# One-core inference step with expert retrieval: the lead-in before the first gather is rebuilt

## The chip, the cores and the metric

The kernel runs on one core of one Trainium2 chip. The metric is the time of one execution in device microseconds (us). Three executions of the kernel before took 3244.26, 3246.60 and 3248.41 us; their median, 3246.6 us, is the time before. One more execution was recorded by the profiler.

Names used for the engines: PE is TensorE (PEld its weight loads), DVE is VectorE, ACT is ScalarE, POOL is GpSimd, SP is SyncE, which only issues DMAs here.

## The reference, cut to what matters

1024 prompt tokens and 64 sample tokens, each 1024 wide, go through one layer, all in float32:

```
x <- LN1(alpha*x + Mixer(x))
x <- LN2(alpha*x + PEER(x))
Mixer: one projection (1024 -> 2048: lru_x 512, lru_gate 512, sc_B, sc_C, sc_x, mem_q 256 each)
  A (512): conv of width 4 -> gated linear recurrence over time -> * gelu(gate)
  B (256): y = B * conv3(C * x_sc)
  C (256, 4 heads): softmax attention into 256 memory tokens (k, v = mem @ w_mem_kv)
  RMSNorm of each group, concatenation, one output projection (1024 -> 1024)
PEER: 8 heads; scores against 2 x 128 keys, top 16 of each half, top 16 of the 256 sums;
  every token gathers 16 experts per head: rows u and v of 1024 floats out of 16384
  out = sum over experts of softmax(score) * gelu(x . u) * v
```

Outputs are x of all tokens, the keys and values of the prompt's memory, and the last states of convolutions and recurrence.

## The kernel before

Tokens are cut into tiles of 128 (8 of the prompt, one half-filled of the sample). **The main loop** runs over 1088 slots. A slot is one gather: POOL issues an indirect DMA (L698) that brings u and v rows for 128 pairs of token and expert, 1 MB, into one of 8 ring buffers of `arena` (`RING`). DVE takes the dot product with the token's x (L1567), ACT makes gelu and weight (L1166 to L1175), and PE adds the weighted v rows into the tile's sum (`combine`, L972, two matmuls). Gather n waits for `used`, the end of `combine(n - 8)`. `replicate` (L956, copied by ACT at L1144) spreads x for the dots, once for 2 slots in the first groups. The indices of a gather come from `keyscores` (L921), `route` on DVE (top 16s, L1449 to L1507), `select` on PE (L941) and `copy_idx` (L1514), for a unit of two heads at a time.

**The mixer** is computed in three blocks of three tiles. Blocks 1 and 2 are mixed into the slots of the main loop. Block 0 (tiles 0 to 2, 384 tokens) has to come first, since no gather can start without x after LN1: its work is the lead-in. It is cut into named stages: `half` and `lx`, `lg`, `qp`, `sx`, `sb`, `sC` (the two halves of a projection of 128 columns, L725), `kv`, `kt`, `kk`, `kc` (memory keys and values), `cv` (convolution), `gr`, `gi`, `sr`, `si`, `ta`, `ra`, `rc`, `sd`, `re` (gates and recurrence), `as`, `mx`, `ex`, `nz`, `at`, `tc`, `av`, `ty` (attention, six rounds r: tile r // 2, half of the heads), `sh` (group B), `sq`, `nm`, `rm`, `no` (RMSNorm of one group: squares, sum by a matmul with ones, root, scaling), `oa`, `ob`, `op` (output projection of one tile and half of the columns; `oa` and `ob` are its parts for tile 0, L849), `z` (residual sum, L1419), `l1`, `dv`, `l2` (layer norm, L1425 to L1437), `xt`, `xe` (transposes, L880), `w0`, `wa`, `wq` (query projections, one side of 16 each, L891: `w0` for tile 0 alone, `wa` and `wq` for more tiles), and `K0`, `T0`, `E0`, `S0`, `I0`, `G0`, `R0`, `C0` (key scores, routing, selection and replication of the first unit).

**The order** is written by hand: `put(engine, step, block, name, arg)` adds a stage to an engine's list, and each list is sorted by step. Steps below 0 (from `LEAD`, -200) are the lead-in, run one stage after another; steps from 0 are slots, and there `PE_PACE` and `DVE_PACE` say how many slots pass between two pieces of a stage. A stage waits by semaphore for the stages that it reads. SP's list holds the loads: weights of a stage go through three buffers `win`, so the load of one waits for the stage three before it (`weight`). ACT issues the first three weights and memT, wkv before its own work.

```
put("pe", v(38), "op", (1, 0))
for side in range(8):
    put("pe", v(40 if side < 4 else 49), "w0", side)
put("pe", v(42), "K0")
for n, (ti, half) in enumerate(((1, 1), (2, 0), (2, 1))):
    put("pe", v(43 + n // 2), "op", (ti, half))
put("pe", v(46), "S0")
```

So all six output projections and both halves of tile 0's stand ahead of `S0` on PE. `w_out` (4 MB) lies in ring buffers 4 to 7, and gather 4 waits for the last `op`.

## Time and profile before

| | |
|---|---|
| median of three executions | 3246.6 us (3244.26 to 3248.41) |
| profiled execution, its own time | 3244.09 us |
| its span | 3242.1 us |
| bytes moved by DMA | 1261.34 MB, mean 389 GB/s |
| PE busy | 2502.6 us (77%), granted clock 0.852 on the mean |
| DVE, ACT, POOL busy | 2143.6, 1410.8, 1234.8 us |
| first gather issued | 233.45 us from the start |

### The profile page before, as it was taken

To read this page: it belongs to the slowest core of one execution; us is meant where nothing else is said; L and a number is where in the kernel's file an instruction comes from. 1 tells how busy PE (TensorE), PEld (TensorE's weight loads), DVE (VectorE), ACT (ScalarE), POOL (GpSimd) and SP (SyncE) were. 2 spreads that over 40 slices of the span, in tenths; PEclk is the share of its full clock that TensorE was granted. 3 is DMA by queue.
4 is the path that set the end of the run, shared out by engine and by line. 5 is a ranking of instruction groups with operands and counts; after the bars stand their busy time and mean duration, and the time that the engine had idled before them with its cause. 6 is when DMAs were issued, how large, how long until landed. Compare 5 with 4: busy or idle time off the path is not lost.

```text
span 3242.1 us, 36014 instructions
## 1 busy us (share of the span) xinstructions
PE 2502.6 (77%) x10100; PEld 722.2 (22%) x10100; DVE 2143.6 (66%) x4901; ACT 1410.8 (44%) x4028; POOL 1234.8 (38%) x1092
## 2 busy tenths in 40 slices
PE   6888998878786898788788868877666666676775
PEld 3543332222111232223222113311111111110010
DVE  2546678888766467787877685656666666664554
ACT  1415445566434434455554353434443444443343
POOL 0004443344444434344334443344344433443342
PEclk9998999999898998899988989976776777767677
DMA  3439999999999999999999999999999999999997
GB/s 126 153 108 391 418 417 419 378 394 406 419 420 416 420 420 418 404 382 419 420 419 412 420 419 420 404 401 421 421 412 421 419 416 404 419 420 421 406 415 321
DMA packets 198615, 1261.34 MB, mean 389 GB/s; under 512 B 24080, under 2 KB 27408, under 8 KB 58512
## 3 DMA queue, kind: packets, MB, share of 16 engines
q0 software_dynamic: 156672, 1140.92, 85.4%
q1 hardware_dynamic: 41024, 113.40, 9.2%
q10 hardware_dynamic: 720, 4.72, 0.4%
q8 instruction: 81, 1.33, 0.2%
q14 instruction: 118, 0.97, 0.1%
HBM read 1241.30 MB, written 17.66 MB: 388 GB/s over the span
## 4 chain that ended last, share of the span: by engine, by line
issue 47%; POOL 31%; PE 13%; DMA 6%; DVE 2%; ACT 1%; POOLq 0%; SPq 0%; DVEq 0%; ACTq 0%
POOL arena L698 31%; DMA arena<-in_uv,idxT 5%; PE ps L972 3%; PE ps L891 3%; PE ps L725 2%; PE ps L956 1%; PE ps L849 1%; DMA consts<-in_consts 1%; DVE arena L1567 0%; POOLq L690 0%; PE ps L746 0%; PE ps L921 0%; DMA arena<-in_wq 0%; PE ps L870 0%; DVE arena L1288 0%
## 5 line engine op out<-in xcount | busy, mean ns | idle before, releaser
L698 POOL DMA_INDIRECT arena<-in_uv,idxT x1088 | 1234.6, 1135 | 1977.0 <-PE ps L972 1679.5
L972 PE MATMUL ps<-arena,wset 128*32 128x512 f32 x4352 | 1387.5, 739 | 654.0 <-ACT wset L1175 602.0
L1567 DVE CUSTOM_DVE_ANT_0 arena<-arena 128x1024 f32<-128x1024 f32 x1088 | 1328.6, 1224 | 821.8 <-DMA arena<-in_uv,idxT 738.7
L1166 ACT ACTIVATE gel<-acts 128x1 f32<-128x1 f32 x1088 | 219.7, 202 | 1361.7 <-DVE acts L1567 1353.6
L972 PEld LDWEIGHTS ps<-arena,wset 128*32 128x32 f32 x4352 | 175.1, 118 | 1589.6 <-ACT wset L1175 1399.5
L1170 ACT ACTIVATE wt<-gel,gT 128x1 f32<-128x1 f32 x1088 | 320.5, 295 | 103.4 <-ACT gel L1166 3.7
L1175 ACT ACTIVATE wset<-arena,wt 128x32 f32<-128x32 f32 x1088 | 349.6, 321 | 36.1
L725 PE MATMUL ps<-arena 128*128 128x384 f32 (+1 forms) x768 | 310.2, 525 | 21.4 <-DMA consts<-in_consts 19.3
L891 PE MATMUL ps<-arena 128*128 128x384 f32 (+3 forms) x896 | 294.1, 458 | 17.1 <-DMA arena<-in_wq 15.5
L956 PE MATMUL ps<-arena 32*128 32x512 f32 x704 | 239.6, 762 | 0.0
L891 PEld LDWEIGHTS ps<-arena 128*128 128x128 f32 x896 | 150.1, 197 | 216.8 <-issue 170.3
L725 PEld LDWEIGHTS ps<-arena 128*128 128x128 f32 x768 | 137.5, 201 | 247.9 <-issue 189.7
L1144 ACT ACTIVATE arena<-ps 128x1024 f32<-128x1024 f32 x176 | 177.3, 1007 | 33.5 <-PE ps L956 33.4
L1166 ACT ACT_TABLE_LOAD x78 | 100.1, 1283 | 5.9 <-DVE acts L1567 4.5
L956 PEld LDWEIGHTS ps<-arena 32*128 32x128 f32 x704 | 61.5, 213 | 161.4 <-issue 159.9
L870 PE MATMUL ps<-arena 128*128 128x512 f32 x160 | 93.8, 669 | 0.0
L1567 DVE DVE_READ_ACCUMULATOR2_ANT acts<- 128x1 f32 x1088 | 90.3, 83 | 0.0
L1449 DVE MAX8 val<-ps 128x8 f32<-128x128 f32 x136 | 40.2, 295 | 32.2 <-PE ps L921 32.0
L849 PE MATMUL ps<-arena 128*128 128x512 f32 x96 | 44.2, 620 | 4.5 <-DVEq L1227 4.5
L941 PE MATMUL ps<-consts,eg 128*32 128x16 f32 x2176 | 37.5, 189 | 12.5 <-issue 12.1
L921 PE MATMUL ps<-arena 128*128 128x128 f32 x256 | 42.6, 317 | 3.2 <-DMA arena<-scratch_q 2.8
L1132 ACT ACT_TABLE_LOAD x34 | 43.6, 1283 | 0.6
(171 smaller groups left out, 1488.3 us busy)
## 6 DMA issues: line engine op xcount, KB each, us to landing
arena<-in_wq SPq DMA_DIRECT2D x56, 512.0 KB
arena<-in_w_in SPq DMA_DIRECT2D x45, 512.0 KB
arena<-in_uv,idxT POOLq DMA_INDIRECT x1088
arena<-in_w_outs SPq DMA_DIRECT2D x16, 512.0 KB
arena<-scratch_q SPq DMA_DIRECT2D x30, 256.0 KB
arena<-in_x_tok SPq DMA_DIRECT2D x9, 512.0 KB, 11.6
scratch_x<-arena SPq DMA_DIRECT2D x9, 512.0 KB, 7.9
arena<-in_w_out SPq DMA_DIRECT2D x1, 4096.0 KB, 12.9
```

The costliest lines, as they stand in the source:

```text
L698: pool.indirect_dma_start(out=ring[n % RING], out_offset=None, in_=A["uv"], in_offset=bass.IndirectOffsetOnAxis(ap=idxT[t % 2][:, col:col ...
L725: last = mm(out_, w_[:, kk, :], x_[:, kk, :], start=kk == 0, stop=kk == KD - 1)
L849: last = mm(o_, x8(zone2, b)[:, k, ti * P:(ti + 1) * P], w_out[:, k, half * HALF:(half + 1) * HALF], start=k == 0, stop=k == 5)
L870: last = mm(bank[MB[ti]], y_, w_[:, k2, :], start=k == 0, stop=k == KD - 1)
L891: last = mm(o_[:, 0:hi - lo], w_[:, k, :], x8(zone2, b)[:, k, lo:hi], start=k == 0, stop=k == KD - 1)
L956: last = mm(xr[:, hf * HALF:(hf + 1) * HALF], sel_s[lo:lo + 32, m_, :], x1b[t % 2][lo:lo + 32, hf * HALF:(hf + 1) * HALF], start=True, sto ...
L972: last = mm(ps[r0:r0 + 32, hf * HALF:(hf + 1) * HALF], wset[n % SETS][:, :], v[:, hf * HALF:(hf + 1) * HALF], start=first, stop=final)
L1144: A_(xrep[g % 2], xr, ACT.Copy).then_inc(xr_cp, 1)
L1166: A_(gel[:, n % COLS:n % COLS + 1], acts[:, n % COLS:n % COLS + 1], ACT.Gelu).then_inc(gelus, 1)
L1170: A_(wt[:, n % COLS:n % COLS + 1], gel[:, n % COLS:n % COLS + 1], ACT.Copy, scale=gT[t % 2][:, col:col + 1]).then_inc(weights, 1)
L1175: A_(wset[n % SETS][:, :], masks[:, m_, :], ACT.Copy, scale=wt[:, n % COLS:n % COLS + 1]).then_inc(sets, 1)
L1567: V.tensor_tensor_reduce(out=ring[n % RING][:, 0:D], in0=ring[n % RING][:, 0:D], in1=xrep[g % 2], scale=1.0, scalar=0.0, op0=ALU.mult, op1 ...
```

## The change

- **Loads.** ACT issues only three weights, now those of `lx 0`, `lx 1`, `qp 0`. SP issues x, par, consts, then wrg, memT, wkv. The small states cvst and scst, which block 2 alone needs, go behind keys and sel.
- **First products.** `half` no longer waits for consts; `kt`, the first stage that reads it, does.
- **Order.** The steps of block 0 are replaced by three written lists, `FIRST_PE`, `FIRST_ACT` and `FIRST_DVE`. Only rounds 0 and 1 of attention come ahead of tile 0's norm; rounds 2 to 5 stand further behind, between later stages. `op` (1, 0) and (2, 0) go behind `R0`, `op` (1, 1) and (2, 1) into slots 0 and 3; `z` of tiles 1 and 2 go to slots 2 to 5 and their layer norms behind them. `wa` starts at slot 18 instead of 9 and has pace 0.33 for 0.5. `w0` 4 to 7 stay behind `S0`.
- **Norms in parts.** `sq`, `nm`, `rm`, `no` of block 0 run for tile 0 (128 columns) first and for tiles 1 and 2 (256) later.
- **Layer norm in parts.** The two `bn_stats` become stages `ls` of their own; `l2` works on halves of 512 columns, and `xt` waits for its half only. This holds for all blocks.
- **Banks.** Attention of block 0 alternates between two PSUM banks (`abank`), `gr` and `gi` use bank 0, `nm` bank 0.
- **Output weights.** `w_out` is loaded as eight pieces into ring buffers 6 and 7, `yout`, `x1b[1]` and the half of `ln` that LN2 uses; gather 6 waits for `op` (2, 0), and LN2's row of `ln` is loaded at slot 20, behind `op` (2, 1).

```diff
+FIRST_PE = """
+    half.lx.0 lx.0 half.lx.1 half.qp.0 gr.0 lx.1 qp.0 kv.0 gi.0 half.lg.0 kv.1 lg.0 gr.1 kt.0 half.lg.1
...
+    half.sb.1 sb.1 half.sx.1 nm.1.0 sx.1 nm.0.0 half.sC.1 sC.1 oa.0.0 nm.2.0 oa.0.1 ob.0.0 ob.0.1 at.2
+    as.3 av.2 xt.0.0 xt.0.1 w0.0 w0.1 at.3 w0.2 av.3 as.4 as.5 w0.3 at.4 K0 av.4 at.5 av.5 nm.1.1 S0
+    w0.4 nm.0.1 w0.5 nm.2.1 w0.6 w0.7 R0 op.1.0 op.2.0
+    """
+FIRST_DVE = """
+    cv.0 kc.0 ra.0 rc.0 cv.1 kc.1 cv.2 re.0 ra.1 rc.1 mx.0 cv.3 mx.1 re.1 nz.0 ra.2 nz.1 rc.2 re.2 ty.0
+    ra.3 rc.3 re.3 ty.1 sh.0 mx.2 no.1.0 no.0.0 nz.2 sh.1 no.2.0 z.0.0 ls.0.0 z.0.1 ls.0.1 l1.0 l2.0.0
+    l2.0.1 ty.2 mx.3 nz.3 ty.3 mx.4 mx.5 nz.4 nz.5 T0 ty.4 ty.5 I0 no.1.1 no.0.1 no.2.1
+    """
...
+    put("pe", 0, 0, "op", (1, 1))
+    put("pe", 3, 0, "op", (2, 1))
+    for i, arg in enumerate(((1, 0), (2, 0), (1, 1), (2, 1))):
+        put("dve", (2, 3, 4, 5)[i], 0, "z", arg)
     for ti in (1, 2):
...
     for side in range(8, SIDES):
-        put("pe", 9 + 4 * (side - 8), "wa", side)
+        put("pe", 18 + 3 * (side - 8), 0, "wa", side)
...
+    w_out = [ring[RING - 2][:, 0:D], ring[RING - 2][:, D:], ring[RING - 1][:, 0:D], ring[RING - 1][:, D:],
+             yout, x1b[1], ln[:, 2 * D:3 * D], ln[:, 3 * D:]]
...
-            if n == 4:
-                after(pool, "pe", 0, "op", (2, 1))
+            if n == RING - 2:
+                after(pool, "pe", 0, "op", (2, 0))
...
             if name == "half":
-                pe.wait_ge(ld["consts"], 16)
                 pe.wait_ge(ld["xT0"], 16 * (b + 1))
```

PE around the first selection, before: one row is a run of equal matmuls; L849 is the output projection, L832 the norm's sum, L880 `xt`, L891 a query side in eight, L921 key scores, L941 the selection, L956 `replicate`, L972 `combine`.

```order
L849 MATMUL ps<-arena 128x512 x12
L832 MATMUL ps<-arena,consts 128x384 x2
L849 MATMUL ps<-arena 128x512 x12
L880 MATMUL ps<-consts,arena 128x128 x8
L891 MATMUL ps<-arena 128x128 x32
L921 MATMUL ps<-arena 128x128 x4
L849 MATMUL ps<-arena 128x512 x24
L941 MATMUL ps<-consts,eg 32x16 x32
L956 MATMUL ps<-arena 128x512 x2
L891 MATMUL ps<-arena 128x128 x32
L956 MATMUL ps<-arena 128x512 x2
L921 MATMUL ps<-arena 128x128 x4
```

The same place after, from the key scores (L911) to the third slot; L931 is the selection, L881 the query sides, L819 the norm's sum, L763 and L774 the attention's transposes and value products, L840 the output projection, L946 `replicate`, L962 `combine`.

```order
L911 MATMUL ps<-arena 128x128 x4
L774 MATMUL ps<-arena 64x128 x4
...
L931 MATMUL ps<-consts,eg 32x16 x32
L881 MATMUL ps<-arena 128x128 x8
L819 MATMUL ps<-arena,consts 128x256 x2
L881 MATMUL ps<-arena 128x128 x8
L819 MATMUL ps<-arena,consts 128x256 x2
L881 MATMUL ps<-arena 128x128 x16
L946 MATMUL ps<-arena 128x512 x2
L840 MATMUL ps<-arena 128x512 x16
...
L840 MATMUL ps<-arena 128x512 x8
L962 MATMUL ps<-arena,wset 32x512 x2
```

The 24 matmuls of `op` that stood between key scores and selection are gone from there; 24 stand between selection and the first `combine`, 8 behind the third.

PE where it works on `wa` in the slots, before (L891 is `wa`, two matmuls to a slot):

```order
L972 MATMUL ps<-arena,wset 32x512 x2
L891 MATMUL ps<-arena 128x384 x2
L956 MATMUL ps<-arena 128x512 x2
L972 MATMUL ps<-arena,wset 32x512 x2
L891 MATMUL ps<-arena 128x384 x2
```

and after (L881 is `wa`):

```order
L962 MATMUL ps<-arena,wset 32x512 x2
L881 MATMUL ps<-arena 128x384 x3
L962 MATMUL ps<-arena,wset 32x512 x2
L881 MATMUL ps<-arena 128x384 x2
L946 MATMUL ps<-arena 128x512 x2
```

Two or three of `wa`'s matmuls now stand between two slots, and nine slots more lie ahead of the first.

## Rows read from the trace of the kernel before

**Rows 1.** The page: the span, and GB/s of DMA in 40 equal slices.
```profile
span 3242.1 us, 36014 instructions
...
GB/s 126 153 108 391 418 417 419 378 394 406 419 420 416 420 420 418 404 382 419 420 419 412 420 419 420 404 401 421 421 412 421 419 416 404 419 420 421 406 415 321
```

**Rows 2.** Stretches: start:end length, busy PE, PEld, DVE, ACT, POOL, clock, DMA share, GB/s.
```profile
0.00:5.00 5.00, 0.00 (x0) 0.00 (x0) 0.28 (x3) 1.28 (x1) 0.20 (x4) 1.00 0.54 189
5.00:10.00 5.00, 0.00 (x0) 0.00 (x0) 0.00 (x0) 0.00 (x0) 0.00 (x0) 1.00 1.05 409
...
19.34:210.50 191.16, 166.62 (x541) 95.26 (x541) 79.41 (x157) 58.80 (x103) 0.00 (x0) 0.94 0.31 111
180.00:188.00 8.00, 4.19 (x5) 1.85 (x6) 3.95 (x4) 0.00 (x0) 0.00 (x0) 0.61 0.00 0
...
253.50:267.20 13.70, 9.04 (x22) 2.00 (x22) 10.97 (x28) 8.08 (x16) 2.27 (x2) 0.50 0.86 316
...
280.00:440.00 160.00, 159.56 (x765) 59.90 (x764) 104.67 (x258) 83.47 (x227) 71.42 (x54) 1.00 1.02 416
440.00:3240.00 2800.00, 2120.41 (x8528) 540.55 (x8526) 1914.77 (x4354) 1244.00 (x3649) 1143.95 (x1019) 0.84 1.00 411
```

**Rows 3.** Waits of PE up to 210.5 us: for what, us in all, times, longest.
```profile
PE ps L725 <- DMA consts<-in_consts: 19.3, 1, 19.3
```

**Rows 4.** DMA issues up to 60 us: count, KB each, median us to landing.
```profile
arena<-in_xT SPq DMA_DIRECT2D x2, 768.0 KB, 6.8
```

**Rows 5.** Chain that ended last, lead-in and first slots: start, us, what, records.
```profile
19.34 13.26 PE ps L725 x32
32.60 6.87 PE ps L746 x16
...
48.92 5.16 PE ps L725 x16
...
57.10 1.06 PE ps L770 x4
...
105.70 1.03 PE ps L789 x8
...
211.66 20.60 PE ps L849 x48
...
282.36 1.49 PE ps L891 x4
283.84 0.98 PE ps L972 x4
...
286.31 1.06 PE ps L956 x4
```

**Rows 6.** In order of time, 196 to 260 us: start, us, engine, line, what.
```profile
196.58 1.04 PE L880 MATMUL ps<-consts,arena 128*128 128x128 f32 x8
...
198.40 3.81 PE L891 MATMUL ps<-arena 128*128 128x128 f32 x32 [0.79 <-DVEq L1227]
...
211.69 0.30 DVE L1449 MAX8 val<-ps 128x8 f32<-128x128 f32 x1 [14.14 <-PE ps L921]
...
228.20 0.19 DVE L1507 TENSOR_TENSOR eg<-eg,den 128x32 f32<-128x32 f32 x1
...
232.19 0.74 PE L941 MATMUL ps<-consts,eg 128*32 128x16 f32 x64
...
233.45 1.07 POOL L698 DMA_INDIRECT arena<-in_uv,idxT  x1 [233.00 <-DVE idxT L1514]
...
235.73 1.29 DVE L1425 BATCH_NORM_STATS2 bst<-arena 128x6 f32<-128x512 f32 x2
...
251.68 1.29 DVE L1435 SCALAR_TENSOR_TENSOR arena<-arena,mv 128x1024 f32<-128x1024 f32 x1
...
256.31 1.21 DVE L1567 CUSTOM_DVE_ANT_0 arena<-arena 128x1024 f32<-128x1024 f32 x1
...
258.16 1.92 PE L972 MATMUL ps<-arena,wset 128*32 128x512 f32 x4 [6.25 <-ACT wset L1175]
```

More of the change, by code:

```diff
@@ L105, in put, with plan_norm @@
     PLAN[eng].append((step, b, name, arg))
+def plan_norm(b, ti, x):
+    for half in range(2):
+        put("dve", x + half / 2, b, "ls", (ti, half))
+    put("dve", x + 1, b, "l1", ti)
+    put("act", x + 3, b, "dv", ti)
+    for half in range(2):
+        put("dve", x + 4 + half / 2, b, "l2", (ti, half))
 def plan_later_block(b):
@@ L464, in build @@
     kbank, xr, ybank = bank[3], ps[:, 6 * 512:8 * 512], ps[:, 0:D]
-    ld = {k: sem("ld_" + k) for k in ("consts", "par", "cvst", "scst", "wrg", "memT", "wkv", "ln", "wout", "keys",
+    ld = {k: sem("ld_" + k) for k in ("consts", "par", "cvst", "scst", "wrg", "memT", "wkv", "ln", "ln2", "wout", "keys",
                                       "sel", "xT0", "xT1")}
@@ L511, in gbank, with span, abank @@
     def gbank(b, name, c):
-        return MB[1] if b == 0 else pbank(b, "lx" if name == "gr" else "lg", c)
+        return 0 if b == 0 else pbank(b, "lx" if name == "gr" else "lg", c)
+    def span(b, part):
+        return (0, cols(b)) if b else ((0, P), (P, cols(0)))[part]
+    def abank(b, r_):
+        return 1 if b == 0 and r_ % 2 else MB[2]
     def nbank(b, g):
-        return MB[1] if g == G_LRU or (b and g == G_SC) else MB[2]
+        return 0 if b == 0 else MB[2] if g == G_MEM else MB[1]
     def q_order(b, k):
@@ L667, in _ @@
             if n == 20:
+                after(sp, "pe", 0, "op", (2, 1))
                 load_x1(1)
+                load("ln2", ln_v[:, 2:4, :], A["ln"][2:4].partition_broadcast(P))
             t = SLOT[n][0]
@@ L827, in run @@
             elif name == "nm":
-                o_ = claim(nbank(b, arg), "act", b, "rm", arg)
-                ks = GROUPS[arg][1]
+                g, part = arg
+                lo, hi = span(b, part)
+                o_ = claim(nbank(b, g), "act", b, "rm", arg)
+                ks = GROUPS[g][1]
                 for i, k in enumerate(ks):
-                    after(pe, "act", b, "sq", k)
-                    last = mm(o_[:, 0:n_], ones, sqb[k][:, 0:n_], start=i == 0, stop=i == len(ks) - 1)
+                    after(pe, "act", b, "sq", (k, part))
+                    last = mm(o_[:, 0:hi - lo], ones, sqb[k][:, lo:hi], start=i == 0, stop=i == len(ks) - 1)
                     if i == len(ks) - 1:
@@ L989, in _ @@
                 select(u)
+            if n == 1:
+                for k in (0, 1):
+                    after(pe, *holder[k])
             if n >= 1:
@@ L1401, in run @@
             elif name == "no":
-                rs = rmsbuf[arg][:, 0:n_]
+                g, part = arg
+                lo, hi = span(b, part)
+                rs = rmsbuf[g][:, lo:hi]
                 after(dve, "act", b, "rm", arg)
@@ L1590, in build @@
         x.__exit__(None, None, None)
-INPUTS = ["consts", "sel", "par", "cvst", "scst", "wrg", "memT", "wkv", "w_in", "xT", "w_out", "w_outs", "ln", "ckT", "cv", "x_tok",
+INPUTS = ["consts", "sel", "par", "cvst", "scst", "wrg", "memT", "wkv", "w_in", "xT", "w_outs", "ln", "ckT", "cv", "x_tok",
           "wq", "keys", "uv"]
```

264 lines of the change are left out of this document (112 added, 152 removed).

## The prediction

> **What bounds the kernel now.** I read the strips first [rows 1]: the first three of 40 slices (243 us) move 108 to 153 GB/s, nearly all others about 420. The table of stretches says the same of the main loop: from 440 us on the DMA share is 1.00 at 411 GB/s with PE at 76% [rows 2]. So the main loop is bound by the gathers' bytes, and the lead-in, in which there is nothing to gather, is bound by something else. An earlier first gather is worth its whole advance only if nothing between it and the DMA-bound part is slower than the DMAs. That is not so here: from 280 to 440 us PE is busy for 159.56 of 160 us at full clock, and the DMA share is 1.02 as well [rows 2]. Slots 16 to 64 are bound by PE and DMA together. The change takes work out of the lead-in and puts it into just that stretch. So the sum has three parts: the first gather, the first `combine`, slot 64.
>
> **The first product.** PE waits 19.3 us for consts, which stand behind x and par in SP's queue while ACT's queue moves 4.7 MB beside them [rows 3]. Now the first product needs a half of x and one weight. The x loads landed a median 6.8 us after their issue at about 1 us [rows 4]; 189 GB/s for 5 us and 409 after [rows 2] give 2.2 MB by 8 us, and what has to be in by then is 0.8 MB of x and the weights beside it (0.5 to 1.6 MB). I take 8.0 us, with 7 and 10 as ends: 11.3 us earlier. The first 32 records took 13.26 us for 10.3 at the later 0.3225 [rows 5], a slow start of 2.9 us that comes in both. DVE's preparation from par and `kv` (memT and wkv now land last; 7.1 MB at 409 GB/s is about 19 us, and PE reaches `kv 0` at about 26) are covered by other products. SP's queue now takes half of ln and the output weights, 5.2 MB or 12.6 us at 415 GB/s, after the seventh weight instead of 7.7 MB after the ninth; the three buffers `win` hold 15.5 us of products meanwhile (3 x 5.16 [rows 5]), so I cost it at nothing, and at up to 5 us if a weight comes late.
>
> **PE's work ahead of the key scores,** after, in order of the list: 128 matmuls of projections at 5.16 / 8 = 0.645 us, 82.6, and 2.9 for the slow start; 8 of the gates, same width, 5.2; `kv` 2 x 6.87 = 13.7; six `as` at 1.06, 6.4; five `at` and one `kt`-like set of four transposes at 0.5 each, 3.0; four `av` at 1.03, 4.1; `oa`, `ob` 16 x 0.859 = 13.7; two `xt` 1.0; four `w0` at 1.9, 7.6 [rows 5, 6]; the eight sums of the norm on 128 columns: no row has them; between the 0.24 of a query side's matmul of that width [rows 6] and the 0.645 of 384 columns [rows 5] I take 0.25, 2.0. Sum 142. Before, `op` (1, 0) (6.9), the wider norms (3.1), one `at` and two `av` (2.6) stood there too: 12.6 us of work gone from in front of the key scores.
>
> **Waits.** Between 19.34 and 210.5 us PE was busy for 166.6 of 191.2 us; 24.6 were idle. The clock was 0.94 on the mean, which is 12% of the time at half speed, up to 11 us more [rows 2]. Where do the waits go? They came from chains that end on DVE or ACT (convolution to gates, softmax to transpose, norm to projection) with the next stage right behind on PE. In the new lists a full product of 2.6 us or more stands between each such pair, attention rounds use two banks, and behind the output projection of tile 0 two rounds of attention cover the layer norm. I laid the three lists side by side with the durations above, each stage beginning when its engine and its inputs are free: PE stays fed but for about 4 us around `xt`. Semaphores and late weights will add some; I allow 8, with 3 and 22 as ends. Half speed follows a wait here (0.61 over 180 to 188 us, around a wait of 4.5 us, and 4.19 us busy) [rows 2], so with the waits most of it goes too. The key scores begin at 8 + 142 + 8 = 158 us, for 210.5.
>
> **To the first gather.** Routing takes from 211.7 to 228.4 us, 16.7; then PE had 3.8 us of `op` to finish before `select` at 232.19, and the gather went out at 233.45, 22.9 after the key scores began [rows 6]. Now nothing is ahead of `select` but done work; two short copies on DVE (`ty`) come in between. 20 us: the first gather at 178, 55 earlier. PE is idle for about 12 us while DVE routes.
>
> **To the first combine.** The output projections were not saved but put behind. From `select`'s end (177.2): 32 matmuls of `w0` 7.6, four norm sums on 256 columns 1.7, key scores 1.0, two `replicate` 2.1, three `op` (two ahead of slot 0, one in it) 20.6 [rows 5, 6], 33.0 in all, and 2.5 for half speed after the idle 12 us: 213, for 258.2 before [rows 6]: 45 earlier. Gathers 6 and 7 wait for `op` (2, 0) and gather 8 for this `combine`, so the DMAs, which need 20 us for eight gathers (1.05 MB at 420 GB/s), run dry for some 15. That costs nothing by itself; the slots are late anyway. The fourth `op` follows in slot 3: 6.9, so 38 earlier.
>
> **Slots 3 to 18.** DVE can't take `z` (2, 1) before this `op`. It then has, before slot 18, 12 dots of 1.3 us (15.6), two layer norms of about 4.5 (stats 1.3, two full-width passes of 1.29 now in halves, small ones) and one routing of 16.7: 41 us [rows 6]. PE has in that time 12 slots at 0.98 + 0.53 and about 4 us besides [rows 5], 22 us: it idles 20. Before, `wa` began at slot 9 and filled these gaps; what PE lost there was 4.7 us idle and 4.5 at half speed between 253.5 and 267.2 [rows 2], about 9. Net 11 lost, bounds 0 and 22: 27 or 28 earlier at slot 18 in PE's work done. From there to 64 PE has the same matmuls at full clock, only bunched by threes: 0.98 + 0.53 + 1.49 = 3.0 us a slot before [rows 5], 3.65 in 24 slots of `wa` now, the total unchanged. From slot 64 the DMAs bound both kernels with the same bytes, and the later blocks are written as before but for the layer norm in halves (about 0.4 us a tile of DVE's time, which isn't the bound).
>
> **Sum:** 55 at the first gather, less 10 to the first `combine`, less 7 for the fourth `op`, less 11 for PE's idle time gives 27 to 28; I take 28. Against the profiled execution's own time, 3244.1 us (span 3242.1), that is 3216.1; this execution lies 2.5 us under the median of 3246.6, so **3218.6 us**, 0.9% faster.
>
> **A rule that would give more.** Page "Perfetto Trace Analysis", section "Optimization Strategy", of the Trainium skill says that where the most contended engine changes over time, interleaving those regimes may improve performance. By it the deferred projections would vanish in the DMA-bound loop and the whole 55 us would stay; the row of 280 to 440 us, PE 159.56 of 160, does not agree, and it decides my sum.
>
> **Rivals.** (a) The whole advance carries, because PE catches up: it would have to find 27 us between the slots. For it: from 440 us PE has a quarter of its time free. Against it: 280 to 440 [rows 2]. 3246.6 - 52 = 3195. (b) The lead-in's new order is bound by its chains after all: ACT or DVE late in one stage holds every later one, as the lists are strictly in order. With the 24.6 us of waits and the slow clock as before, the first gather is only some 30 earlier and the gain 3 to 8: 3241. For it: DVE has reciprocals of 2.5 us a stage, and 79 us of work in 191 [rows 2] leaves slack; that speaks against it. (c) Slower: TensorE's clock stays at its lower level in the thin slots. The stretch 253.5 to 267.2 shows 0.50 with PE two thirds busy [rows 2]. Between first `combine` and slot 18 PE is now no busier, and if the lower level holds while `wa` runs, each slot costs up to 3.6 us more. From 8 such slots on the gain is gone; 12 give 3262. Against it: 280 to 440 ran at 1.00, and `wa` keeps PE full. Page "TensorE: Matmul & The Clock Gate" of the Trainium skill, section "Why this matters for your kernels", advises against idle gaps between bursts of matmuls since they bring the lower clock back; by that the 12 us of idle during routing, which the old order filled with `op`, speak against this change. The row of 180 to 188 us agrees. (d) It does what it says up to slot 64, but PE enters block 1 at slot 72 late, and its chains give the gain back: within 6 us of 3246.6.
>
> **Chances.** Forecast 0.68 (3203 to 3237 with its terms at their ends), (a) 0.09, (b) 0.13, (c) 0.04, (d) 0.06. The range 3201 to 3238 takes in the forecast's ends and the nearer parts of (a) and (b). A measurement of this kernel tells about 0.2% (6.5 us) from no change: faster 0.87, same 0.08, slower 0.05.
>
> **What would show it.** First matmul at 8 us, key scores at about 158, first gather at 178, PE idle for about 12 us before `select`, first `combine` at 213, then gaps on PE up to about slot 18, slot 64 some 28 us earlier than before, and the strips from slice 6 on as before, shifted. Wrong at the root would be a first gather later than 195, a clock of 0.5 beyond slot 18, or an advance at slot 64 that is not the advance at the end.

## The result and the profile after

The changed kernel takes 3226.6 us (median of 4 runs, 3223.6 to 3231.9); the kernel before, beside it on the same chip, 3247.1. The medians are 20.6 us apart. The ratio is 0.9932 (95% interval 0.9917 to 0.9946), so the kernel is 0.7% or about 22 us faster. A second group of runs gave 3222.1 for 3249.0, ratio 0.9924 (0.9910 to 0.9937). The prediction was 3218.6 in a range of 3201 to 3238. The profiled execution of the first group took 3231.9 us, the longest of its four; the second profile (3218.9 us of span, called "again" below) helps to tell what belongs to the program and what to one execution.

The page of the changed kernel, against [rows 1]:

```profile
span 3230.1 us, 36070 instructions
...
GB/s 211 124 215 384 390 414 378 375 393 393 420 421 416 421 419 418 396 390 415 419 419 412 420 411 420 403 396 421 421 413 421 421 416 413 421 417 421 405 418 320
```

The third slice (161 to 242 us) moves 215 GB/s for 108: here the gathers run already. Slices 7 and 8 are weaker than before (378, 375 for 419, 378). The table of stretches of the changed kernel, columns as in [rows 2]:

```profile
8.00:160.00 152.00, 145.78 (x500) 87.03 (x500) 70.81 (x153) 51.01 (x102) 0.00 (x0) 0.97 0.45 162
...
215.00:262.00 47.00, 39.23 (x122) 9.89 (x120) 36.12 (x91) 25.41 (x57) 18.06 (x15) 0.81 0.84 334
262.00:440.00 178.00, 172.00 (x814) 66.69 (x812) 113.83 (x298) 84.78 (x234) 71.08 (x57) 0.98 0.99 390
```

In the lead-in PE is busy for 145.8 of 152 us at a clock of 0.97; before, it was 166.6 of 191.2 at 0.94 [rows 2]. The 24.6 us of idle time are down to 6. Of the waits of the kernel before, beside the one in [rows 3], these were the longest (what for, us, times, longest): for attention's softmax and its transposes, and for the norm ahead of the output projection.

```profile
PE ps L770 <- DVE arena L1381: 6.3, 3, 5.2
PE ps L778 <- DVEq L1227: 6.0, 2, 4.4
PE ps L849 <- DVEq L1227: 4.5, 1, 4.5
```

What PE still waits for after, up to 185 us:

```profile
PE ps L931 <- DVE eg L1509: 11.5, 1, 11.5
PE ps L710 <- DMA arena<-in_xT: 7.8, 1, 7.8
PE ps L870 <- DVEq L1222: 2.8, 2, 1.7
PE ps L710 <- DMA arena<-in_w_in: 2.4, 1, 2.4
```

The first product waits for x alone (7.8 for 19.3), the selection waits 11.5 us for the routing, and one weight was 2.4 us late. The lists, the norms in parts and the two banks came together; no run separates them. In order of time (start, us, what), for PE and then for POOL, against [rows 5, 6]:

```profile
160.64 1.06 PE L911 MATMUL ps<-arena 128*128 128x128 f32 x8
...
178.57 1.05 PE L931 MATMUL ps<-consts,eg 128*32 128x16 f32 x64 [11.51 <-DVE eg L1509]
179.55 3.60 PE L881 MATMUL ps<-arena 128*128 128x128 f32 x16
...
191.12 2.02 PE L881 MATMUL ps<-arena 128*128 128x128 f32 x16 [2.67 <-DMA arena<-in_wq]
...
210.12 7.03 PE L840 MATMUL ps<-arena 128*128 128x512 f32 x16
217.08 1.05 PE L962 MATMUL ps<-arena,wset 128*32 128x512 f32 x4
```

```profile
180.16 1.07 POOL L683 DMA_INDIRECT arena<-in_uv,idxT  x1 [179.71 <-DVE idxT L1516]
...
208.91 0.93 POOL L683 DMA_INDIRECT arena<-in_uv,idxT  x1 [21.26 <-PE ps L840]
```

Key scores at 160.6 (210.5 before), first gather at 180.2 (233.4), gather 6 at 208.9 behind `op` (2, 0), first combine at 217.1 (258.2), gather 8 behind it at 218.4.

**The advance by slots.** How far each gather starts ahead of the same one before, in us, from the profiled executions (starts of line 698 before, of the `DMA_INDIRECT` line after):

| slot | before, at | after | again | before_first | before_loads | gap_filled | early_tail |
|---|---|---|---|---|---|---|---|
| 0 | 233.4 | 53.3 | 54.0 | 9.9 | 9.5 | 53.9 | 55.6 |
| 8 | 260.4 | 41.9 | 42.7 | 9.2 | 9.1 | 45.8 | 34.1 |
| 18 | 285.1 | 39.0 | 39.7 | 9.2 | 9.1 | 42.9 | 31.3 |
| 48 | 376.7 | 26.2 | 27.1 | 9.2 | 9.1 | 30.4 | 10.2 |
| 64 | 423.8 | 27.2 | 28.2 | 9.2 | 9.1 | 31.4 | 8.6 |
| 96 | 513.9 | 21.9 | 23.2 | 9.9 | 8.2 | 26.5 | 10.7 |
| 104 | 536.1 | 17.6 | 23.3 | 9.7 | 8.1 | 26.5 | 8.1 |
| 192 | 794.0 | 12.4 | 24.1 | 6.8 | 3.5 | 26.5 | 9.0 |
| 1087 | 3211.1 | 12.4 | 24.4 | 7.1 | 2.7 | 24.5 | 7.9 |

54 us at the first gather are 28 at slot 64 and, where the execution is not disturbed further, 23 to 24 from slot 96 to the end.

PE's place is seen by the starts of the `combine`s. From the first to that of slot 3 the advance falls by 0.3 us in both profiles, from slot 3 to 18 by 4.8 or 4.9, from slot 18 to 64 by 9.8 or 10.1. The stretch from slot 3 to 18, before and again:

```profile
269.00:308.00 39.00, 38.07 (x136) 11.67 (x138) 31.93 (x78) 25.48 (x67) 22.30 (x15) 1.00 1.01 410
```

```profile
227.50:271.00 43.50, 35.00 (x110) 7.94 (x110) 37.18 (x84) 29.60 (x64) 17.26 (x15) 0.73 0.91 357
```

PE is idle for 8.5 us there, and much of its work runs at the lower level: the mean clock is 0.73 for 1.00.

**The same by bytes.** Four stretches of before, after and again, in this order:

```profile
0.00:180.00 180.00, 143.56 (x444) 79.98 (x444) 69.90 (x149) 57.56 (x96) 0.20 (x4) 0.96 0.37 138
180.00:440.00 260.00, 238.63 (x1130) 101.64 (x1130) 158.94 (x400) 109.22 (x283) 90.65 (x70) 0.94 0.83 334
440.00:800.00 360.00, 298.35 (x1398) 93.76 (x1396) 297.41 (x739) 202.78 (x523) 153.55 (x126) 0.95 1.00 401
800.00:3180.00 2380.00, 1788.74 (x7038) 442.51 (x7036) 1586.14 (x3561) 1019.52 (x3062) 978.20 (x880) 0.82 1.01 415
```

```profile
0.00:180.00 180.00, 153.53 (x606) 93.58 (x607) 88.75 (x223) 56.37 (x110) 0.20 (x4) 0.94 0.42 152
180.00:440.00 260.00, 243.56 (x1064) 96.33 (x1063) 165.23 (x415) 117.93 (x310) 96.97 (x80) 0.95 0.92 364
440.00:800.00 360.00, 300.43 (x1363) 96.22 (x1364) 284.08 (x683) 200.42 (x507) 142.84 (x119) 0.92 0.98 387
```

```profile
0.00:180.00 180.00, 153.76 (x609) 93.91 (x610) 89.43 (x223) 56.45 (x110) 0.74 (x5) 0.95 0.42 152
180.00:440.00 260.00, 242.47 (x1061) 95.39 (x1060) 165.85 (x416) 119.27 (x311) 98.22 (x80) 0.95 0.93 365
440.00:800.00 360.00, 300.71 (x1398) 96.70 (x1398) 294.45 (x710) 206.19 (x523) 150.55 (x125) 0.95 0.99 399
```

The last column is GB/s. Up to 440 us the kernel before moves 0.138 x 180 + 0.334 x 260 = 111.7 MB, again 122.3 MB. These 10.6 MB at the later 415 GB/s are 25.5 us; with 2 GB/s less from 440 to 800 (1.7 us) that makes 23.8, and the table reads 24.1 at slot 192. For the first profile: 10.4 MB, 24.9 us, less 14 GB/s x 360 us = 5.0 MB, 12.1 us, leaves 12.8; the table reads 12.4. The same sum for the eleven other profiles of this document (bytes moved up to 800 us beyond those of the kernel before, divided by 415 GB/s) comes within 1 us of the advance at slot 192 each time, from 4.3 for 3.5 (before_loads) to 27.4 for 26.5 (gap_filled). It is an account and not a cause: all kernels move the same 1261.4 MB, and from 800 us on the two kernels compared here move them at the same 415 GB/s. What it tells is where the time goes: the end is early by the bytes that were moved early, less what is lost between 440 and 800 us (2 us in again, 12 in the first profile).

### The profile page after: what moved, and what is told of

Read it like the earlier page. It is cut to its first block, busy times and chain, and to the rows that moved or that the text cites. A ratio compares the mean times of both kernels' runs of the same rounds, so it can differ in the third digit from the quotient of the medians.

```text
span 3230.1 us, 36070 instructions
## 1 busy us (share of the span) xinstructions
PE 2527.2 (78%) x10116; PEld 730.5 (23%) x10116; DVE 2148.6 (67%) x4930; ACT 1407.9 (44%) x4036; POOL 1221.2 (38%) x1092
## 4 chain that ended last, share of the span: by engine, by line
issue 43%; POOL 28%; PE 14%; DMA 6%; DVE 6%; ACT 3%; POOLq 0%; DVEq 0%; ACTq 0%; SPq 0%
POOL arena L683 28%; DMA arena<-in_uv,idxT 4%; PE ps L962 3%; PE ps L710 3%; PE ps L881 3%; DVE arena L1571 2%; PE ps L946 1%; DMA scratch_q<-arena 1%; PE ps L840 1%; ACT L1161 1%; PE ps L911 1%; DMA arena<-scratch_q 0%; PE ps L730 0%; POOLq L675 0%; DMA arena<-in_w_in 0%
## 5 line engine op out<-in xcount | busy, mean ns | idle before, releaser
L683 POOL DMA_INDIRECT arena<-in_uv,idxT x1088 | 1221.0, 1122 | 1978.2 <-PE ps L962 1717.8
L962 PE MATMUL ps<-arena,wset 128*32 128x512 f32 x4352 | 1404.7, 748 | 625.2 <-ACT wset L1170 559.3
L962 PEld LDWEIGHTS ps<-arena,wset 128*32 128x32 f32 x4352 | 175.9, 119 | 1574.7 <-ACT wset L1170 1325.1
L881 PE MATMUL ps<-arena 128*128 128x384 f32 (+3 forms) x896 | 294.2, 460 | 12.3 <-DMA arena<-in_wq 10.9
L946 PE MATMUL ps<-arena 32*128 32x512 f32 x704 | 243.5, 773 | 0.7 <-ACT arena L1141 0.6
L881 PEld LDWEIGHTS ps<-arena 128*128 128x128 f32 x896 | 152.5, 199 | 207.6 <-issue 165.6
L710 PEld LDWEIGHTS ps<-arena 128*128 128x128 f32 x768 | 139.4, 203 | 245.9 <-issue 190.6
L946 PEld LDWEIGHTS ps<-arena 32*128 32x128 f32 x704 | 62.5, 217 | 165.4 <-issue 158.3
L860 PE MATMUL ps<-arena 128*128 128x512 f32 x160 | 93.4, 667 | 0.0
L931 PE MATMUL ps<-consts,eg 128*32 128x16 f32 x2176 | 39.1, 190 | 25.9 <-issue 14.1
L911 PE MATMUL ps<-arena 128*128 128x128 f32 x256 | 43.4, 321 | 6.5 <-DMA arena<-scratch_q 6.5
L911 PEld LDWEIGHTS ps<-arena 128*128 128x128 f32 x256 | 36.7, 221 | 34.7 <-issue 25.7
L931 PEld LDWEIGHTS ps<-consts,eg 128*32 128x32 f32 x2176 | 32.4, 115 | 48.6 <-issue 36.4
```

The source lines that it names most:

```text
L683: pool.indirect_dma_start(out=ring[n % RING], out_offset=None, in_=A["uv"], in_offset=bass.IndirectOffsetOnAxis(ap=idxT[t % 2][:, col:col ...
L710: last = mm(out_, w_[:, kk, :], x_[:, kk, :], start=kk == 0, stop=kk == KD - 1)
L860: last = mm(bank[MB[ti]], y_, w_[:, k2, :], start=k == 0, stop=k == KD - 1)
L881: last = mm(o_[:, 0:hi - lo], w_[:, k, :], x8(zone2, b)[:, k, lo:hi], start=k == 0, stop=k == KD - 1)
L911: last = mm(kbank[:, si * NK:(si + 1) * NK], qs[:, si * P:(si + 1) * P], keysT[:, a_:a_ + NK], start=True, stop=True)
L946: last = mm(xr[:, hf * HALF:(hf + 1) * HALF], sel_s[lo:lo + 32, m_, :], x1b[t % 2][lo:lo + 32, hf * HALF:(hf + 1) * HALF], start=True, sto ...
```

## The experiments

All in groups with the kernel before on the same chip; times are medians, ratios carry their 95% interval. Advances are of the profiled executions.

**after_again**: the changed kernel, unchanged.

> The changed kernel once more, unchanged, as the measure for the others of this group. In its profiled execution the advance over the kernel before was 53 us at the first gather, 42 at slot 8, 27 at slot 64 and 12 from slot 192 on. Two theories on the 15 us given back between slots 64 and 192. Structural: block 1's projections, which start at slot 72, meet queries of block 0 that end later, and the loss comes again: advance at slot 192 between 10 and 15 us. Variation: that execution (3231.9 us, the slowest of four, whose median is 3226.6) lost some of it to stretches at half clock, and the new profile shows 17 or more at slot 192. Time 3224 to 3229 us by either.

3222.1 us for 3249.0. The advance at slot 192 was 24.1 us, so variation it was for 11 of the 15 us, and the structural part is 4 us (5 at slot 96). Where did the other 11 go? The first profile was 1.3 us behind at slot 96, took 4.3 us more for slots 96 to 104 (26.4 for 22.1), 2.8 more for slots 104 to 176 and 3.2 more for slots 176 to 192; from there to the end both take the same. The first profile from slot 96 to 104 with its inner stretch, then again (columns as above):

```profile
492.00:518.40 26.40, 24.23 (x137) 8.29 (x136) 17.02 (x42) 15.76 (x41) 9.76 (x8) 0.81 0.95 373
...
496.90:507.10 10.20, 10.20 (x84) 3.41 (x82) 7.73 (x17) 8.10 (x22) 2.98 (x3) 0.50 1.01 414
507.10:518.00 10.90, 10.90 (x45) 3.76 (x44) 4.09 (x16) 4.02 (x13) 5.67 (x5) 1.00 0.87 321
```

```profile
490.70:512.80 22.10, 19.59 (x137) 6.97 (x136) 17.26 (x42) 15.60 (x41) 11.77 (x9) 1.00 1.01 417
```

The same 137 records: at half clock (0.50) for 10.2 us PE is busy without a gap and the DMAs fall to 321 GB/s behind it; at 1.00 they don't. Here a stretch at half clock where PE is nearly full costs bytes, and it comes in one execution and not in the other. Over slots 176 to 192 the clock was 0.93 for 1.00 as well; over slots 104 to 176 it was 0.94 in both, and what took 2.8 us there is not known.

**before_first**: the kernel before with only the part on the first product.

```diff
             if name == "half":
-                pe.wait_ge(ld["consts"], 16)
...
             elif name == "kt":
...
                 after(pe, "dve", b, "kc", MC - 1)
+                pe.wait_ge(ld["consts"], 16)
...
         load("wrg", wrg_v, A["wrg"])
+        load("memT", memT, A["memT"])
+        load("wkv", wkv, A["wkv"])
...
-        act.dma_start(memT, A["memT"]).then_inc(ld["memT"], 16)
-        act.dma_start(wkv, A["wkv"]).then_inc(ld["wkv"], 16)
```

> The kernel before with one part of the change alone: the first products don't wait for the constants, and the memory's operands go into SyncE's queue behind the gates' weights instead of ScalarE's queue behind the first three weights. The order of the stages is the old one. My sum's term: first product at 8 us for 19.3, first gather 10 to 11 us earlier than 233.5. It is a pure shift, every later stage stands as before. Theory that a shift is carried: 10 us at slot 64, at slot 192 and at the end, 3237 us. Rival, that the DMA-bound part takes an advance away, whatever its origin (half of it, as for the whole change): 5 us at the end, 3242. Second rival: the key and value products come early in the old order and wait for their operands, which now land at about 19 us: the lead-in gains under 5 us.

3237.0 us for 3249.0, ratio 0.9965 (0.9951 to 0.9979). First product at 7.5 us, 9.9 us at the first gather, 9.2 at slot 64 and 9.9 at slot 96: a pure shift is carried whole into the DMA-bound part. The profiled execution has 7.1 of them left at the end; the medians are 12 us apart. Neither rival held; `kv` waited 0.9 us for its operands.

**before_loads**: the same without the dropped wait, so the loads' order alone.

```diff
         load("wrg", wrg_v, A["wrg"])
+        load("memT", memT, A["memT"])
+        load("wkv", wkv, A["wkv"])
...
-        act.dma_start(memT, A["memT"]).then_inc(ld["memT"], 16)
-        act.dma_start(wkv, A["wkv"]).then_inc(ld["wkv"], 16)
```

> The kernel before with the loads' part alone: the memory's operands in SyncE's queue behind the gates' weights instead of ScalarE's, while the first products still wait for the constants. before_first, which has this and the dropped wait, brought the first product from 19.3 to 7.5 us and the first gather 9.9 us forward. Theory that what held the constants back was the 3.1 MB of the memory's operands moving beside them: first product at 9 to 12 us, so most of the 10 us comes from the loads' order and the dropped wait is worth 2 to 4; time 3239 to 3242. Rival, that the constants are late in any case, being the last small load of their queue: first product at 16 or later, time 3245 to 3249.

3242.4 us for 3250.4, ratio 0.9977 (0.9967 to 0.9987). PE's first wait in before_loads, then in before_first:

```profile
PE ps L727 <- DMA consts<-in_consts: 11.9, 1, 11.9
```

```profile
PE ps L727 <- DMA arena<-in_xT: 7.5, 1, 7.5
```

The constants come 7.4 us earlier when the memory's 3.1 MB no longer move beside them, and the dropped wait gives 4.4 more at the first product. At `xt`, the transposes of tile 0, the two are 7.8 and 9.9 us ahead of the kernel before; at the first gather 9.5 and 9.9. What brings before_loads level stands between: the query sides of tile 0, in the kernel before and then in before_loads.

```profile
204.69 5.44 PE L891 MATMUL ps<-arena 128*128 128x128 f32 x32 [2.48 <-DMA arena<-in_wq]
```

```profile
195.87 2.02 PE L893 MATMUL ps<-arena 128*128 128x128 f32 x16 [1.41 <-DMA arena<-in_wq]
198.58 2.02 PE L893 MATMUL ps<-arena 128*128 128x128 f32 x16 [0.69 <-DMA arena<-in_wq]
```

With one wait of 2.5 us (2.6 in before_first) the 32 records behind it took 5.4 us, with two short waits 4.0. Up to 222 us before_first has 1.3 us more of waits behind its first product (0.9 of them for `wkv`), and PE is busy for 188.5 us in it for 185.4 with the same matmuls, at clocks of 0.94 and 0.95. So the loads' order alone gives 7.4 us at the first product and 7.8 at `xt`; the rest of its 9.5 us at the gathers is seen in one execution, and whether it belongs to the edit is not shown. The two ratios overlap; that the dropped wait is worth something at the end is not shown.

**gap_filled**: query sides in the time in which PE waits for the routing.

```diff
-    ... K0 av.4 at.5 av.5 nm.1.1 S0
-    w0.4 nm.0.1 w0.5 nm.2.1 w0.6 w0.7 R0 op.1.0 op.2.0
+    ... K0 av.4 at.5 av.5 nm.1.1 w0.4
+    w0.6 w0.7 S0 nm.0.1 w0.5 nm.2.1 R0 op.1.0 op.2.0
```

(and the same move of the three evictions ahead of `E0` in `FIRST_ACT`.)

> The changed kernel with three of the last four query sides of tile 0 (w0.4, w0.6, w0.7, 1.9 us each) moved into the 11.5 us in which TensorE waits for the routing, ahead of the selection. Theory of the sum (TensorE and DMA bind together up to slot 64, so work moved into idle time counts in full): wait ahead of the selection 6 us instead of 11.5, first gather unchanged at 180, first combine about 6 us earlier than in the changed kernel, at 211, and 6 us earlier at slot 64; at the end 6 us less than the changed kernel if nothing later takes it, 3 if half is given back. Rival: the weights of these sides are not in yet at 165 us (their loads are behind others in SyncE's queue), so the selection waits for them: first gather 3 to 8 us later and no gain.

3219.8 us for 3249.0, ratio 0.9910 (0.9894 to 0.9925), beside 0.9924 of the changed kernel. PE in order of time:

```profile
166.33 5.52 PE L881 MATMUL ps<-arena 128*128 128x128 f32 x48
178.00 1.06 PE L931 MATMUL ps<-consts,eg 128*32 128x16 f32 x64 [6.15 <-DVE eg L1509]
...
188.58 15.67 PE L840 MATMUL ps<-arena 128*128 128x512 f32 x32 [3.27 <-DVEq L1222]
...
213.19 1.05 PE L962 MATMUL ps<-arena,wset 128*32 128x512 f32 x4
```

The weights were there, the wait ahead of the selection is 6.15 for 11.51 us, and the first gather has not moved. But of 5.4 us filled 3.1 arrive at the first combine (213.2; again 216.3): `op` (1, 0) now waits 3.3 us for DVE's norms, a new wait in place of the 2.8 for a weight. The 3.1 us stay up to slot 96. That is half of the theory's 6. At the last gather this execution is 24.5 us ahead, again 24.4.

**early_tail**: all output projections ahead of slot 0, the rest of the tail earlier.

```diff
-    ... w0.7 R0 op.1.0 op.2.0
+    ... w0.7 R0 op.1.0 op.2.0 op.1.1 op.2.1
...
-        x = (5, 10)[ti - 1]
+        x = (4, 8)[ti - 1]
...
-        put("pe", 18 + 3 * (side - 8), 0, "wa", side)
+        put("pe", 15 + 3 * (side - 8), 0, "wa", side)
...
-    plan_queries(0, 44, 3)
+    plan_queries(0, 40, 3)
```

> The changed kernel with all four output projections of tiles 1 and 2 ahead of slot 0, the layer norms at slots 4 and 8 instead of 5 and 10, the query sides wa from slot 15 instead of 18 and wq from 40 instead of 44. First combine and gather 8 come up to 7 us later than in the changed kernel (225 us for 217), but no projection is left for slot 3, so slot 18 should be level again. Theory that late queries cause the give-back in block 1 (stores of queries, their reloads and block 1's input arrive late): waits of TensorE for reloaded queries and for x in slots 64 to 192 (6.9 and 7.6 us) fall under 3, and the advance lost between slots 64 and 192 falls from 15 to under 8: time 3218 to 3222. Rival, that the give-back has another cause (clock, bytes, or mere variation): the same time as the changed kernel within 3 us, or up to 5 more.

3238.2 us for 3249.0, ratio 0.9968 (0.9955 to 0.9980): 16 us slower than the changed kernel, beyond what either theory gave. It keeps 34.1 us at slot 8 (gather 8 at 226, as expected), but is not level again at slot 18 (31.3 for 39.7) and has 8.6 left at slot 64. Behind slot 64 it does what the first theory said: PE waits 3.3 us for x and for no reloaded query, and nothing is given back (9.0 at slot 192). But it also came there 20 us later than again, so this doesn't tell whether the waits or the later start is the reason.

**early_loose**: early_tail with ScalarE's evictions of the query sides, and the stores behind them, one slot later in their lists.

```diff
-        put("act", 15 + 3 * (side - 8) + 3, 0, "wa", side)
+        put("act", 15 + 3 * (side - 8) + 4, 0, "wa", side)
...
-        put("act", x + each * (side + 1), b, "we", side)
+        put("act", x + each * (side + 1) + (b == 0), b, "we", side)
```

> The kernel of early_tail with one change: ScalarE's evictions of block 0's query sides stand one slot later in its list. early_tail was at 415 us at slot 64, the changed kernel at 396; from slot 16 (248 for 239) to 56 it lost 11 us more, with TensorE 8 us idle, and ScalarE 51 us waiting for query sides for 35. Theory that ScalarE's strict order causes this (an eviction planned before TensorE has finished the side holds GELU, weights and copies of the slots behind it): ScalarE's wait falls to 40 or less, slots 16 to 56 take 136 us or less instead of 144, time 3227 to 3231. Rival, that the query products themselves are at fault (their weights arrive late or TensorE has no room): slots 16 to 56 take 142 to 146 us, time 3236 to 3240.

3228.9 us for 3249.4, ratio 0.9943 (0.9930 to 0.9957). Slots 16 to 56 took 136.4 us for 144.3. What ACT waits for in that stretch, `wa` (L1109) and the copies for the dots (L1139), in early_tail and in early_loose:

```profile
ACT arena L1109 <- PE ps L879: 50.8, 8, 7.4
...
ACT arena L1139 <- PE ps L944: 0.7, 2, 0.4
```

```profile
ACT arena L1109 <- PE ps L879: 33.5, 8, 6.3
...
ACT arena L1139 <- PE ps L944: 13.2, 12, 2.7
```

With the `we` evictions (9.9 and 1.7 us) ACT's waits for PE are 61.4 us and 48.4: 26 us less for query sides, 12.5 more for the copies. Time, wait and stretch came out as the theory of ScalarE's strict order said (136.4 for "136 or less"): the eviction stood where PE had not finished, and the GELU and the weights of the next slots stood behind it in ACT's list.

**gap_loose**: gap_filled with the evictions and the stores one slot later, by the same edit.

> gap_filled with ScalarE's evictions of block 0's query sides one slot later in its list, which took 9 us off early_tail (3238.2 to 3228.9). In the changed kernel ScalarE waited 35 us for these sides between slots 16 and 64, in the kernel before 20 us over a like stretch. Theory that the same strict order costs the changed kernel time too: slots 16 to 56 take 131 us or less for 134, time 3215 to 3218 against 3219.8 of gap_filled. Rival, that it was a fault of early_tail's crowded plan alone (its first side began behind its due slot) and the sides of the changed kernel are on time: the same time within 2 us, or 1 to 3 more since the stores of queries come a slot later.

3220.7 us for 3250.4, ratio 0.9906 (0.9892 to 0.9920). ACT's wait in slots 16 to 56, in gap_filled and in gap_loose:

```profile
ACT arena L1111 <- PE ps L881: 35.0, 8, 5.8
...
ACT arena L1141 <- PE ps L946: 7.9, 9, 2.0
```

```profile
ACT arena L1141 <- PE ps L946: 36.0, 15, 4.0
...
ACT arena L1111 <- PE ps L881: 4.9, 3, 2.1
```

The wait for the query sides is 30 us shorter, but the wait for `replicate`, also PE's work, is 28 us longer, and slot 56 stands at the same 369.7 us. The waits have moved and not gone: for PE's products of all kinds ACT waits 45.1 us and 41.7. The time is what the rival said (the same within 2 us); its reason, that the sides were on time, doesn't fit a wait of 35 us. In both PE is busy for 128.3 of 134 us in that stretch and the DMA share is 0.99 and 0.98, so there was hardly time for an edit of ACT's list to win; in early_tail PE was busy for 128.3 of 144.3 at a share of 0.94.

**x_early** and **queries_42**: the two late transfers of slots 64 to 80, each mended by itself.

```diff
-    put("sp", o - 6, b, "xT")
+    put("sp", o - (22 if b == 1 else 6), b, "xT")
```

> The changed kernel with the load of block 1's x issued at slot 50 instead of 66. In its second profile the advance over the kernel before fell from 28.2 us (slot 64) to 24.1 (slot 192 and on), and TensorE waited there 5.3 us for this x and 6.6 us for reloaded queries. Theory that these late transfers are the structural part of the give-back: the wait for x goes, 2 to 4 us more advance at slot 192, time 3218 to 3220 against 3222 for the changed kernel. Rival: the DMA-bound stretch gives nothing for a shorter TensorE wait, since the gathers' ring is refilled in either case: same time, within 1.5 us.

```diff
-    plan_queries(0, 44, 3)
+    plan_queries(0, 42, 3)
```

> The changed kernel with the query sides wq begun at slot 42 instead of 44, as in the kernel before, so that the store of these queries and their reload for tile 1 come two slots (6 us) earlier. Theory of late transfers: TensorE's wait for reloaded queries (6.6 us) falls under 2, 2 to 5 us more advance at slot 192: time 3217 to 3220. Rival: the sides are then behind the pace of ScalarE's evictions, which hold GELU and sets behind them, and slots 42 to 64 lose 2 to 5 us: time 3223 to 3227.

PE's waits in again from slot 64 to 88, then in x_early from slot 52 to 64:

```profile
PE ps L911 <- DMA arena<-scratch_q: 6.6, 2, 5.9
PE ps L710 <- DMA arena<-in_xT: 5.3, 2, 4.2
```

```profile
PE ps L881 <- DMA arena<-in_wq: 8.2, 1, 8.2
```

x_early: 3230.4 us for 3249.4, ratio 0.9944 (0.9930 to 0.9958). The wait for x is gone and PE waits 8.2 us for a query weight instead: both go through SyncE's queue, and 1.5 MB of x now stand ahead of it. Before the edit has any effect, at slot 48, this execution is 4.1 us behind again (norm_short, below, tells why); at slot 64 it is 13.6 behind and at slot 96 4.4. So the edit is worth nothing by slot 96, neither way; the time lies outside what theory and rival gave. queries_42: 3224.0, ratio 0.9927 (0.9914 to 0.9941). The wait for reloaded queries is 3.9 us, 23.1 us of advance at slot 64 and 24.0 at slot 96. The 5 us that it was behind at slot 64 were back by slot 96 as well. Between slots 64 and 96 PE's place hardly matters; the ring of gathers makes up for it. The rival of queries_42 holds in its time, and "late transfers cost 4 us" falls as a cause that these two edits can mend.

**gap_x_42**: the three edits together.

> Three edits of the changed kernel together: query sides in the routing gap (gap_filled, 2.3 us alone), block 1's x at slot 50, wq from slot 42. If the three are independent and late transfers are the structural give-back: 2.3 + 3 + 3, time 3213 to 3217. If the DMA-bound stretch absorbs the last two: 3218 to 3221, as gap_filled.

3222.1 us for 3249.4, ratio 0.9923 (0.9909 to 0.9937), a little over the second range and no better than gap_filled. PE again waits long for a query weight, 8.6 us; at slot 68 the advance is 17.3 us (gap_filled 31.0), at slot 96 24.4 (26.5).

**two_short** and **norm_short**: whose work sets the pace between slots 0 and 24? two_short leaves out 12 matmuls of PE: two output projections sum only two of their eight slices. norm_short leaves out DVE's work: the last passes of two layer norms cover 32 of 512 columns. Neither computes the right output.

```diff
+                if arg in ((1, 1), (2, 1)):
+                    ks = [0, 5]
                 for k in ks:
```

> The changed kernel with 12 matmuls left out of the part that was put behind the first gather: the output projections (1, 1) and (2, 1) sum two of their eight slices, so columns 512 to 1023 of tokens 128 to 383 are not the reference's. TensorE has 5.3 us less ahead of the first combine and 5.3 less in slot 3. Theory of my sum, that TensorE sets the pace from the selection up to slot 48: first combine 5.3 us earlier (211), and 10 to 11 us at slots 18 and 64 and at the end, 3211 to 3213. Rival, that DVE sets the pace of slots 3 to 18 (40 us of dots, layer norms and routing): only the first 5.3 us are seen at slot 64, 3216 to 3218. Second rival, that the chains behind absorb it (half clock on a thinner TensorE): under 3 us.

```diff
-                c_ = slice(hf * HALF, (hf + 1) * HALF)
+                c_ = slice(hf * HALF, hf * HALF + (32 if b == 0 and ti else HALF))
```

> The changed kernel with DVE's two passes of the layer norm cut to 32 of 512 columns for tiles 1 and 2 (eight instructions of 0.75 us, about 0.6 us less each, 4.5 to 5 us in all); the rest of these tiles' x1 and what is computed from it is not the reference's. Counterpart of two_short, in which 10.5 us less of TensorE's work made slots 8 to 64 only 1.9 us shorter. From the gather of slot 8 to that of slot 24 the changed kernel took 48.3 us (217.6 to 265.9), to that of slot 64 178.0 us. Theory that DVE sets the pace of this stretch: 4 to 5 us less to slot 24, kept at slot 64, time 3217 to 3219. Rival, that it is the chain through the copies and combines whatever either engine has to do (TensorE half busy at half clock, 0.63 over slots 16 to 24): less than 1.5 us, time 3221 to 3223.

two_short: 3218.7 us for 3250.4, ratio 0.9897 (0.9882 to 0.9912). norm_short: 3224.9 for 3246.0, ratio 0.9937 (0.9922 to 0.9951). The profiled executions show it by stretch. From gather 8 to gather 64: again 178.0 us, two_short 176.1, norm_short 174.9. The 5.3 us taken from PE in slot 3 made 1.9. The eight passes of DVE fell from 0.75 us each to 0.25, so 4.0 us were taken (not the expected 4.8), and they made 3.1; up to gather 24 alone it is 1.9 and 2.1, between norm_short's theory and its rival. So neither engine is the bound there alone, and DVE seems the nearer to it, with one profile for each; the price of PE's work in slot 3 is about a third of its duration. Two_short's other 5.3 us stand ahead of the first combine, and there the clock has to be told first. In norm_short gather 6 came 5 us later than in again though nothing was changed before it. PE's stretches from 190 to 202 us, again and norm_short:

```profile
190.00:196.00 6.00, 5.66 (x26) 3.41 (x27) 1.47 (x3) 1.46 (x3) 0.00 (x0) 1.00 1.03 423
196.00:202.00 6.00, 6.00 (x15) 2.66 (x14) 0.91 (x2) 1.94 (x4) 0.00 (x0) 1.00 0.82 344
```

```profile
190.00:196.00 6.00, 3.88 (x20) 3.11 (x20) 0.02 (x1) 0.28 (x1) 0.00 (x0) 0.76 1.01 421
196.00:202.00 6.00, 6.00 (x13) 2.32 (x10) 2.38 (x4) 3.12 (x5) 0.00 (x0) 0.67 1.00 413
```

The same instructions, once at 1.00 and once at 0.76 and 0.67, both behind a wait for a weight (2.8 us in again, 3.7 in norm_short). From gather 0 to gather 6 the changed kernel and its variants with the old gap took 28.8, 28.7, 32.9, 32.0, 32.2, 33.1, 32.0 and 30.6 us in their eight profiled executions (after, again, x_early, queries_42, two_short, norm_short, early_tail, early_loose). The three kernels with the gap filled (gap_filled, gap_x_42, gap_loose) took 25.4, 25.4 and 25.4.

Between gather 6 and gather 8, which waits for the first combine, stands the shortened projection: two_short took 4.3 us there, after, again, norm_short, x_early and queries_42 9.5 each. So the 5.3 us ahead of the first combine count in full. With the 1.9 us that makes some 7 us, between the theory's 10 to 11 and the rival's 5; the ratios' difference (0.9897 to 0.9924, 9 us) says the same within its interval. In norm_short the 3.1 us don't show in the time, since the late gather 6 took them.

## Why the prediction came out as it did

**First product: right, its cause only in part.** 8.0 us forecast, 7.8 measured. I argued from the wait for constants; before_loads shows that their lateness was itself the loads' doing: the loads' order alone gives 7.4 of the 11.8 us at the first product, and the dropped wait 4.4.

**The lead-in: right.** 142 us of work and 8 of waits gave 158 for the key scores; it was 160.6, with 7.2 us of waits behind the first product (2.4 of them a weight that I had costed at nothing, up to 5) and 145.6 us of work at the clock that it had. The clock was 0.97 for 0.94. Rival (b) is out. First gather 180.2 for 178; PE's idle time at the routing 11.5 for 12.

**First combine: 217.1 for 213.** 2.4 of these 4 us were lost before: `select` ended at 179.6 for 177.2. The way from there took 37.5 us for 35.5: with the work at its 33 us, the half speed behind the idle time is left with 1.9 us where I had allowed 2.5, and PE waited 2.7 us for a weight that I had costed at nothing. 41 us earlier, not 45.

**From there to slot 64: the sum right, its terms not.** I took 7 us for the fourth projection and 11 for the idle time around it, 18 in all; the loss from gather 8 to slot 64 was 14.5 (42.7 to 28.2). The term that was too large is the fourth projection at its full 6.9: PE's work in slot 3 weighs about a third (two_short). I had the reason in my own sum (DVE's 41 us beside PE's 22 in slots 3 to 18) and still charged both. The idle time itself was mis-sized too: PE was idle for 8.5 us in slots 3 to 18 and not for 20, since its clock was 0.73 and the same work took longer. By stretch 0.3 us went up to slot 3, where I had charged 7, and 14.6 from there to slot 64, where I had charged 11. The kernel before took 10.9 us from its first combine to that of slot 3, the changed one 11.2 with the projection in it. The two errors, 4 at the combine and 4 the other way here, cancel by luck, so slot 64 is 28.2 (27.2 in the first profile) for 28.

**"From slot 64 the DMAs bound both": 4 us too good.** 28.2 at slot 64 are 23.2 at slot 96 and 24.4 at the end. PE waits 12 us there for reloaded queries and for x, where the kernel before waited 2.8 for queries; but mending either changed nothing by slot 96. By bytes it can be told, if not explained: PE's place at slot 64 is not the DMAs' place. The changed kernel had filled 10.6 MB more by 440 us, which are 25.5 us, and at the bound only that is left. This is rival (d) in kind, at a fraction of its size: 4 us, where (d) gives back 22 or more. The first profiled execution lost 11 us more up to slot 192; for 7.5 of them the clock was lower than in again (0.81 for 1.00 over slots 96 to 104, 0.93 for 1.00 over slots 176 to 192). I had no term for such variation.

**Rivals (a) and (c).** (a) is out: nobody caught up. Of (c) a part is true: from 215 to 262 us the clock was 0.81, and 0.73 from slot 3 to 18, but from 262 to 440 us, with `wa` running, 0.98, so nothing was added slot by slot.

The 8 us between 3218.6 and 3226.6 are thus 4 from behind slot 64, and the rest lies within what two groups of runs differ by (ratios 0.9932 and 0.9924, 2.6 us, each with an interval of 4.5 us either way).

**A version that may be better.** gap_filled and gap_loose (0.9910 and 0.9906) stand against 0.9932 and 0.9924, but gap_x_42, with the gap filled too, has 0.9923. The intervals overlap, so a gain at the end is not shown. What is seen in all three profiles of this kind is that gather 6 comes 3 to 8 us sooner behind gather 0. The Trainium skill, page "TensorE: Matmul & The Clock Gate", section "Why this matters for your kernels", advises against idle gaps between bursts. The trace agrees in part: 25.4 us each time with the gap half filled, 28.7 to 33.1 without. But 3.3 us of that stand against the two profiles without a clock loss at 190 to 202 us, and come from the moved work; and with the gap filled the clock fell there too, to 0.89 to 0.95.

## What to carry to other kernels

When a kernel ends in a long DMA-bound loop, price a change to its lead-in by the bytes that it lets through before the loop becomes DMA-bound: take GB/s times length of the early stretches, and divide the difference by the later rate. An advance of a stage in time is worth that only if it is a shift of everything behind it (before_first had 9.2 of its 9.9 us at slot 64 and 9.9 at slot 96); work put behind the first gather is paid back in the stretch where the engines are full, but only as far as that engine is the one that is late. And when an edit shortens one wait of an engine, look at its other waits in the same stretch: in gap_loose 30 us less for one product of PE came back as 28 us more for another, and nothing was won; in early_loose 13 us of ACT's waits for PE really went, and the stretch was 8 us shorter.
